# A decoder layer with attention, state space and experts: moved diagonals, all-ones router sums, one meeting fewer

## The reference

```python
def post_norm_block(x, mix, w_out, ln1_g, ln1_b, w_router, b_router, w_gate, w_up, w_down, ln2_g, ln2_b):
    h = layer_norm(ALPHA * x + mix @ w_out, ln1_g, ln1_b)
    f = moe(h.reshape(-1, D_MODEL), w_router, b_router, w_gate, w_up, w_down).reshape(h.shape)
    return layer_norm(ALPHA * h + f, ln2_g, ln2_b)

def moe(h, w_router, b_router, w_gate, w_up, w_down):
    aff = jax.nn.sigmoid(h @ w_router)                   # 16 experts in 4 groups
    biased = aff + b_router
    gscore = lax.top_k(biased.reshape(n, 4, 4), 2)[0].sum(-1)
    gsel = jnp.argmax(gscore, axis=-1)                   # the best group, then its best two experts
    _, idx = lax.top_k(jnp.where(in_group, biased, NEG_INF), 2)
    w_sel = jnp.take_along_axis(aff, idx, axis=-1)
    gates = one_hot(idx) * w_sel / w_sel.sum(-1)
    hid = silu(h @ w_gate) * (h @ w_up) * gates          # per expert
    return sum over experts of hid @ w_down
```

## Time and profile before

| | us |
|---|---|
| median of 3 runs | 1010.66 (1008.32 to 1015.02) |
| the profiled execution | 1010.17 |
| its span, first to last instruction | 1008.4 |
| PE busy in the span | 920.7 (91%) |
| DVE, ACT, POOL busy | 433.8, 322.1, 215.6 |
| mean granted clock of PE | 0.975 of full |

### The profile page before, as it was taken

One profiled execution on the slowest core, in us unless ns is written; L12 is line 12 of the kernel. 1 busy time (PEld: TensorE's weight loads), 2 busy tenths in 40 slices (PEclk: granted clock), 3 DMA queues, 4 the chain that ended last, 5 costly groups with the idle time before them and its releaser, 6 DMA issues. The chain is left out here.

```text
span 1008.4 us, 13949 instructions
## 1 busy us (share of the span) xinstructions
PE 920.7 (91%) x5113; PEld 584.3 (58%) x5113; DVE 433.8 (43%) x1305; ACT 322.1 (32%) x652; POOL 215.6 (21%) x300
## 2 busy tenths in 40 slices
PE   4999999889999999998899999995699999999695
PEld 4656546555556665565654454542688787878331
DVE  4689699613444344446423326648000100010156
ACT  6751506603233233336323234331212121211222
POOL 3088000002002247731201000423000000000065
PEclk9999999999999999999999999998799999999898
DMA  9540000454983026318332121475866888966294
GB/s 228 164 169 1 2 0 21 132 172 140 424 336 108 1 89 202 110 42 310 131 107 60 40 71 44 168 285 200 288 234 246 287 333 277 378 231 251 69 387 161
DMA packets 63855, 173.91 MB, mean 172 GB/s; under 512 B 17432, under 2 KB 26703, under 8 KB 58279
## 3 DMA queue, kind: packets, MB, share of 16 engines
q1 hardware_dynamic: 55047, 141.37, 39.9%
q0 software_dynamic: 8544, 31.07, 8.5%
q10 hardware_dynamic: 192, 0.52, 0.2%
HBM read 113.76 MB, written 59.24 MB: 172 GB/s over the span
## 5 line engine op out<-in xcount | busy, mean ns | idle before, releaser
L1491 PE MATMUL banks<-xT,arena 128*128 128x384 f32 (+1 forms) x384 | 125.5, 483 | 7.2 <-DVE mx L1702 4.1
L2171 PE MATMUL banks<-arena,mixT 128*128 128x512 f32 x288 | 132.0, 605 | 0.0
L1491 PEld LDWEIGHTS banks<-xT,arena 128*128 128x128 f32 x384 | 72.2, 192 | 58.4 <-DVE mx L1702 11.5
L2171 PEld LDWEIGHTS banks<-arena,mixT 128*128 128x128 f32 x288 | 53.3, 194 | 56.2 <-issue 56.2
L1610 ACT ACTIVATE arena<-arena,mx 128x128 f32<-128x128 f32 (+8 forms) x72 | 58.5, 813 | 75.8 <-DVE mx L1702 75.2
L2335 PEld LDWEIGHTS banks<-mixT,v_tok 128*128 128x128 f32 x512 | 72.0, 194 | 4.5 <-issue 4.5
L2335 PEld LDWEIGHTS banks<-mixT,arena 128*128 128x128 f32 x512 | 70.4, 190 | 6.8 <-issue 6.8
L2335 PE MATMUL banks<-mixT,v_tok 128*128 128x160 f32 x512 | 72.6, 303 | 0.8 <-ACT mixT L2553 0.8
L2335 PE MATMUL banks<-mixT,arena 128*128 128x160 f32 x512 | 71.7, 300 | 0.8 <-ACT mixT L2553 0.8
L2706 POOL DMA_INDIRECT arena<-y_park,slot_s x18 | 17.1, 949 | 258.0 <-DMA y_park<-arena 252.8
L2980 DVE TENSOR_TENSOR mixT<-arena,banks 128x320 f32<-128x320 f32 x16 | 7.8, 487 | 130.5 <-PE banks L2335 130.5
(11 more groups left out here) (412 smaller groups left out, 1379.7 us busy)
## 6 DMA issues: line engine op xcount, KB each, us to landing
arena<-in_w_down SPq DMA_DIRECT2D x16, 1024.0 KB, 8.7
x_slots<-xT SPq DMA_DIRECT2D x4, 2048.0 KB, 13.6
y_park<-xT SPq DMA_DIRECT2D x4, 2048.0 KB, 31.4
v_tok<-in_w_gate SPq DMA_DIRECT2D x8, 1024.0 KB, 5.8
v_tok<-in_w_up SPq DMA_DIRECT2D x8, 1024.0 KB, 5.5
arena<-in_w_gate SPq DMA_DIRECT2D x8, 1024.0 KB, 5.0
arena<-in_w_up SPq DMA_DIRECT2D x8, 1024.0 KB, 8.7
arena<-x_slots SPq DMA_DIRECT2D x16, 512.0 KB, 5.4
```

The source lines that it names most:

```text
L1491: last = T.matmul(b[:, 0:cn], w[:, k, :], xT[:, k, c0:c0 + cn], start=(k == 0), stop=(k == KD - 1))
L2171: last = T.matmul(bank[half], mixT[:, k, t * P:(t + 1) * P], w_oh[half][:, k, :], start=(k == 0), stop=(k == KD - 1))
```

## The change

Six edits, in the order of the program:

1. `phase` gets an argument. The front ends with the block's own barrier alone: no clearing and no second barrier. `made` runs on, and the attention phase clears the semaphores of both.
2. `gain_sums` makes two products with `all1` (a 128 x 128 matrix of ones) as weights: one over `w_rg` (gain times router weight, 256 columns with padding), one over the new `w_rb` (shift times router weight, 128 columns). DVE makes `w_rb`, and sums over k afterwards with two reductions in place of one copy. The call moves behind the second quarter, and PE waits there for POOL's `all1` and DVE's two tables.
3. For tile 8 the residual is added in two halves inside `measure`: the first half after the second quarter (`s_mh`), then its statistics, then the second half.
4. For tile 8 DVE, not POOL, adds the shift, right behind `gained` and ahead of `slots(3)`; the last scatter and SP wait for `s_hv`.
5. ACT makes `scaled_i` and the 18 `dg` ahead of the overflow block, behind its last two stores of expert rows, where it used to make them behind the block. Two waits for the last even expert stand ahead of them.
6. In the final stage the last tile uses whole tiles: 128 rows and columns of the scaled identity, and 64 columns of each diagonal, where it used 80, 64 and 16.

```diff
         @contextmanager
-        def phase():
-
-            made.clear()
+        def phase(clear=True):
+
             with ExitStack() as mem:
                 with nc.Block() as block:
                     yield mem, block
-            nc.clear_and_free_semaphores(list(made))
-            nc.all_engine_barrier()
+            if clear:
+                nc.clear_and_free_semaphores(list(made))
+                nc.all_engine_barrier()
+                made.clear()
...
-        with phase() as (mem, block):
+        with phase(clear=False) as (mem, block):
...
+            w_rb = mem.enter_context(nc.sbuf_tensor("w_rb", [P, KD, E], F32))[:, :, :]
...
+                    if t == NT - 1 and quarter == 1 and k == KD - 1:
+                        last.then_inc(s_mh, 1)
...
                 def gain_sums():
-                    for n in range(2):
-                        for k in range(KD):
-                            last = T.matmul(bank[B_LG][:, E * n:E * (n + 1)], gcol[:, n, k:k + 1].to_broadcast([P, P]),
-                                            w_r[:, k, :], start=(k == 0), stop=(k == KD - 1))
-                    last.then_inc(s_gs, 1)
+                    pe.wait_ge(s_pc, 3)
+                    pe.wait_ge(s_gk, 2)
+                    T.matmul(bank[B_LG][:, 0:KD * 32], all1, w_rg[:, :, :].rearrange("p k e -> p (k e)"),
+                             start=True, stop=True)
+                    T.matmul(bank[B_LG][:, KD * 32:KD * 32 + KD * E], all1, w_rb.rearrange("p k e -> p (k e)"),
+                             start=True, stop=True).then_inc(s_gs, 1)
...
-                    if t == 0:
-                        gain_sums()
-                    else:
+                    if t >= 1:
                         route_parts(t - 1)
                     if dec and t % 2 == 0:
                         turn_keys(d, 1)
                     project(t, 1)
+                    if t == 0:
+                        gain_sums()
...
-                        T.matmul(duo[t % 4][rows, cols], scaled_i[rows, rows], h_all[rows, t, cols],
+                        T.matmul(duo[t % 4][:, cols], scaled_i, h_all[:, t, cols],
                                  start=True, stop=False)
...
-                            w = min(HP, TOK - t * P - HP * g)
-                            last = T.matmul(duo[t % 4][HP * g:HP * g + w, cols], dg[t][g][:, 0:w], y[s][:, cols],
+                            last = T.matmul(duo[t % 4][HP * g:HP * (g + 1), cols], dg[t][g], y[s][:, cols],
                                             start=False, stop=True, tile_position=(0, HP * g))
...
-                act.wait_ge(s_tb, 1)
-                act.wait_ge(s_yo[0], 16 * E // 2)
-                overflow(act, lambda: act.sem_inc(s_oA, 1), body, lambda n: act.wait_ge(s_of, n * NT + 1))
-
+                act.wait_ge(s_gt, E - 1)
+                act.wait_ge(s_up, E - 1)
                 S.activation(scaled_i, ident[:, :], ACT.Copy, scale=ALPHA).then_inc(s_al, 1)
                 act.wait_ge(s_stk, 1)
                 act.wait_ge(s_si2, 1)
                 for t in range(NT):
                     for g in range(2):
                         S.activation(dg[t][g], stack_i[:, :], ACT.Copy, scale=wst[:, t, g:g + 1]).then_inc(s_dg, 1)
+                act.wait_ge(s_tb, 1)
+                act.wait_ge(s_yo[0], 16 * E // 2)
+                overflow(act, lambda: act.sem_inc(s_oA, 1), body, lambda n: act.wait_ge(s_of, n * NT + 1))
...
                 def measure(t):
                     s = t % 3
-                    dve.wait_ge(s_res, t + 1)
-                    V.bn_stats(ln[s][:, 0:6], h_all[:, t, 0:512])
+                    if t < NT - 1:
+                        dve.wait_ge(s_res, t + 1)
+                        V.bn_stats(ln[s][:, 0:6], h_all[:, t, 0:512])
+                    else:
+                        dve.wait_ge(s_mh, 1)
+                        chain(V.scalar_tensor_tensor(h_all[:, t, 0:512], h_all[:, t, 0:512], ALPHA, duo[0][:, 0:512],
+                                                     ALU.mult, ALU.add))
+                        V.bn_stats(ln[s][:, 0:6], h_all[:, t, 0:512])
+                        dve.wait_ge(s_mm, t + 1)
+                        V.scalar_tensor_tensor(h_all[:, t, 512:1024], h_all[:, t, 512:1024], ALPHA, duo[0][:, 512:1024],
+                                               ALU.mult, ALU.add).then_inc(s_res, 1)
+                        dve.wait_ge(s_res, t + 1)
                     chain(V.bn_stats(ln[s][:, 6:12], h_all[:, t, 512:1024]))
...
                 choose(3)
                 gained(NT - 1)
+                dve.wait_ge(s_gn, NT)
+                V.tensor_tensor(h_all[:, NT - 1, :], h_all[:, NT - 1, :], gb[:, 1, :], ALU.add).then_inc(s_hv, 1)
                 slots(3)
```

26 lines of the change are left out of this document (18 added, 8 removed).

## The result

The changed kernel takes 1003.25 us (median of 8 runs, 998.46 to 1004.22), the kernel before 1009.58 (median of 8, 1006.81 to 1015.02): a ratio of 0.9928, interval 0.9903 to 0.9953. Its profiled execution has a span of 1001.6 us in place of 1008.4, 6.8 less.

What follows compares the result with a forecast made beforehand. PE, busy for 91% of the span, was taken to bound the kernel. The terms -1.25 + 0.67 - 1.7 - 4.5 + 0.2 + 0 - 1.5 = -8.1 us, from 1010.17, gave 1002.0, range 999.0 to 1007.0.

Steps and rivals of the forecast that it cites:

- Meeting: Front's end: without the second barrier PE starts 1.2 us earlier; -1.25 us with the entry of its sequencer.
- clock behind it: Behind the front's end: PE's idle is halved, the clock stays full; -1.7 us, bounds -1.7 and 0.
- first rival: Half-clock stretch stays behind the front's end or router sums: 1003.7 us with one, 1005.4 with both; chance 0.22.
- Longer clear: Attention phase's end: clearing 156 semaphores in place of 35 takes about 890 ns; +0.67 us on every engine's path.
- Router sums: Tile loop: two products replace 32 records, -2.8 us, and the clock behind them stays full, -1.7; together -4.5.
- Split: Tile 8's residual in halves: no half starts earlier, turn(8) starts later; +0.7 us, bounds 0.64 and 0.81.
- Shift: Tile 8: the addition in DVE's row costs +1.25 us; DVE's stall in slots(3) goes with POOL's addition, -1.80.
- Diagonals: Experts' end, on ACT: PE never waited for them but may wait for the release; 0 us, bounds 0 and +0.9.
- just in time: Experts' end: ACT's release of PE comes at about 956.2, PE starts residual at 956.37; 0 us lost.
- its other estimate: Experts' end: with ScalarE's queue of eight, ACT's release comes a microsecond earlier than by four; nothing is lost.
- Last tile: Final stage: tile 8's products take 1.94 us in place of 4.00; limited by DVE, -1.5 us comes through.
- third rival: Another half-clock stretch, at the experts' start or in the final stage, is shorter: 1.7 us less, 1000.3; chance 0.13.

Runs made afterwards that it cites:

- front_alone: The kernel before with only the front's second barrier and its clear removed (one meeting): 1007.25 us, ratio 0.9981.
- fill_both: Changed kernel with diagonals moved back, tile 8 reordered, front semaphores cleared early, 12 idle products before the experts, six behind: 992.04 us, ratio 0.9845.

## Why the prediction was right

The forecast was 1002.0 in a range of 999 to 1007; 1003.25 was measured, and 6.3 us of gain between the medians (6.8 between the two profiles) where the sum had 8.1. By its steps:

- **Meeting, clock behind it**: -1.25 and -1.7; the idle fell by 1.24 and the 96 products by 1.70, the latter in all eleven kernels with one meeting (29.75) and in none of the three with two (31.45). The first rival, that the clock is not given back, did not come at either place.
- **Longer clear**: +0.67; the clear grew by 0.65, POOL's entry to it from 105 to 292 ns, PE's idle by 0.84 (1.69 to 2.53).
- **Router sums**: -4.5; -4.51. Here the number is in part luck: 2.84 is the products, and the other 1.67 is the clock behind them, which `front_alone` has back with the old sums.
- **Split**: +0.7; +0.79. **Shift**: 1.25 - 1.80 = -0.55; -0.69. POOL's addition is the cause of the stall, shown both ways. The trace agrees with the rule of the Trainium skill, "SBUF — State Buffer", section "SBUF: two separate sides", on which the prediction drew: only the operation with both inputs in SBUF stalls, until POOL's ends.
- **Diagonals**: 0 for PE, and 0 it is, but not "just in time". ACT's release came at 949.0, 2.0 us ahead of the end of its last diagonal (946.69 + 4.39) and 1.9 ahead of PE's wait for it at 950.9. When the load of the count began, at 948.3, eleven of the 18 diagonals had not started; the sum went by four, its other estimate by eight. And I looked for what waits for ACT's release alone, and not for what the moved instructions had stood in front of: **the table load**, +1.34, is the cost that the sum lacks.
- **Last tile**: -1.5; -1.66 (28.11 to 26.45 once the load is out of the way), of which the changed kernel shows 0.32, because the load takes the rest. The forecast's 1.54 is a slip: its rows give 995.01, and so 1.58. No run takes this edit alone.

The edits so add up to -1.24 - 1.70 + 0.84 - 4.51 + 0.79 - 0.69 + 1.34 - 1.66 = -6.8, the whole difference of the spans. The parts that belong to no single edit nearly cancel in this pair of executions: the fall at 241 (+1.5) and that at the turn (+0.8; it came with the new sums and a long stand, at +0.2 to +0.8) against earlier rows at the experts' start (-1.1) and a shorter half-clock stretch in the final stage (-1.1). The -1.1 at the experts' start may be the change's in part: the kernel before and the three built on it have 15.54 to 16.11 there, the changed one and those built on it 13.33 to 15.24; which edit does it is not shown. By its edits the sum is 1.3 us too large, which is the table load; that the parts of no edit cancel, so that the time came out no further off, is luck. The mechanisms of meeting, split, shift and last tile, and the products of the sums, are what was forecast. The third rival, shorter stretches elsewhere, thus came true in part, beside a new one that had no name.

## What to carry to other kernels

When instructions are moved out of a place, ask what the next instruction there has to carry: a wait, a table load, a release; here a move worth nothing in itself uncovered 1.3 us. A half finished earlier is worth something only if the engine that makes it is free then: the split lost 0.8 us in its old row and won once `slots(2)` stood behind it. Compare executions by stages, from row to row: differences of 1 us in one edit are plain there, in stages that do not jump by themselves, where a median of runs that scatter by 5 us shows none.

## What the runs showed of the hardware that was not expected

The clock's falls to half are not a fixed property of a program. Behind the same short waits at 240 to 242 the same products ran at half clock in six of the fourteen profiles and at full clock in the others; of the kernels alike up to there, those with the fall need 1.2 to 1.8 us more for the phase (261.28 and 261.85 against about 260.1). The tile loop's start shows the same (with the new sums 179.50, about 181.0 or 182.23 us). Products that only keep PE busy gave back 1.4 to 3 us behind the experts (9.12 in place of 10.55 to 12.14 us), and cost nothing while PE's sequencer went through the overflow block, whose branch took 4.11 us in the earlier trace rows: in `fill_both` it ran from 935.2 to 939.4, and PE's products beside it until 938.6. A clear of semaphores takes time by their number: 221 ns for 35, 697 for 121, 721 for the 126 of the last phase, 874 for 156. A load of ACT's function table can carry a wait: the same 1.28 us stood 12 us ahead of their use, or behind the wait for it, by what came ahead of the load.
